# Layer 1's mixer: modulation by width quarters, part of the projections in unsplit fp32, pooling as band products

## The reference

```
mod = silu(c) @ w_ada + b_ada                    # 2048 -> 12288, one row of c
sh1, sc1, gt1, sh2, sc2, gt2 = split(mod, 6)
h = rmsnorm(x, g) * (1 + sc1) + sh1
proj = h @ w_in                                  # 2048 -> 3072
xr, gr, xp = proj[:, :1024], proj[:, 1024:2048], proj[:, 2048:]
xr = causal_dwconv(xr, w_conv, b_conv)           # 4 taps
r, i = sigmoid(xr by heads @ w_rg_a + b), sigmoid(xr by heads @ w_rg_i + b)
a = exp(8 * r * log_sigmoid(lam)); u = sqrt(1 - a*a) * i * xr
hr = scan over tokens of (a, u)
y_lru  = hr * gelu(gr)
y_pool = ((causal mean of xp over 2, 4, 8, 16 tokens) - xp) by groups @ w_pool * ls_pool
x = x + gt1 * (concat(y_lru, y_pool) @ w_out)    # 2048 -> 2048
h = rmsnorm(x, g2) * (1 + sc2) + sh2             # then the gated feed-forward, width 5632
```

## Time and profile before

| | us |
|---|---|
| median of 3 runs (2688.2 to 2691.19) | 2690.42 |
| the profiled execution's own time | 2695.73 |
| its span | 2694.0 |
| PE busy in the span | 2485.4 (92%) |
| DVE busy | 1874.6 (70%) |
| ACT busy | 1140.8 (42%) |
| POOL busy | 257.4 (10%) |
| DMA | 639.05 MB, mean 237 GB/s |

### The profile page before, as it was taken

One profiled execution on the slowest core, in us unless ns is written; L12 is line 12 of the kernel. 1 busy time (PEld: TensorE's weight loads), 2 busy tenths in 40 slices (PEclk: granted clock), 3 DMA queues, 4 the chain that ended last, 5 costly groups with the idle time before them and its releaser, 6 DMA issues.

```text
span 2694.0 us, 34697 instructions
## 1 busy us (share of the span) xinstructions
PE 2485.4 (92%) x13534; PEld 2160.7 (80%) x13534; DVE 1874.6 (70%) x1808; ACT 1140.8 (42%) x1303; POOL 257.4 (10%) x418
## 2 busy tenths in 40 slices
PE   1189788999999999999999999888999999999999
PEld 1188767888888888888999998787888888888887
DVE  5778788788888888767776445765578755555565
ACT  2053533534433443455335555433454444444443
POOL 2312611011111111100110000000001000000000
PEclk9599899999999999999999999999999999999999
DMA  9887778688888888855995555234568755555554
GB/s 333 297 303 258 257 271 311 223 308 322 308 307 307 309 307 302 286 188 172 343 324 172 163 166 157 80 116 149 197 229 306 251 189 187 190 193 193 187 181 148
DMA packets 290575, 639.05 MB, mean 237 GB/s; under 512 B 21754, under 2 KB 34556, under 8 KB 290076
## 3 DMA queue, kind: packets, MB, share of 16 engines
q1 hardware_dynamic: 236112, 440.61, 48.6%
q0 software_dynamic: 53792, 196.63, 20.0%
q10 hardware_dynamic: 556, 0.18, 0.0%
HBM read 635.28 MB, written 2.10 MB: 237 GB/s over the span
## 4 chain that ended last, share of the span: by engine, by line
PE 80%; DVE 9%; DMA 4%; ACT 2%; issue 2%; POOL 2%; DVEq 0%; POOLq 0%; ACTq 0%
PE PS L1569 79%; DMA R<-in_w_ada 4%; DVE R L964 3%; DVE WLO L944 2%; ACT WHI L516 1%; DVE R L1463 1%; POOL YF L461 1%; PE PS L1745 1%; POOL YF L460 0%; PE PS L1710 0%; POOL YF L465 0%; DVE H L989 0%; POOL R L467 0%; DVE R L1291 0%; DVE R L1032 0%
## 5 line engine op out<-in xcount | busy, mean ns | idle before, releaser
L944 DVE TENSOR_TENSOR WLO<-RAW,WHI 128x1024 fp32r<-128x1024 f32 x816 | 1004.2, 1233 | 695.3 <-ACT WHI L516 693.3
L516 ACT ACTIVATE WHI<-RAW 128x1024 fp32r<-128x1024 f32 x816 | 863.3, 1060 | 1247.8 <-PE PS L1569 1247.5
L1569 PE MATMUL PS<-WHI,H 128*128 128x512 f32 x3488 | 1088.9, 393 | 29.8 <-DVE WLO L944 19.2
L1569 PEld LDWEIGHTS PS<-WHI,H 128*128 128x128 f32 x3488 | 654.1, 189 | 172.1 <-issue 22.2
L1569 PE MATMUL PS<-WLO,H 128*128 128x512 f32 x1744 | 682.9, 392 | 0.0
L1569 PE MATMUL PS<-H,WHI 128*128 128x256 f32 x3168 | 593.7, 289 | 42.3 <-DVE WLO L944 36.4
L1569 PEld LDWEIGHTS PS<-H,WHI 128*128 128x128 f32 x3168 | 503.8, 196 | 52.9 <-DVE WLO L944 43.7
L964 DVE SCALAR_TENSOR_TENSOR R<-R,CA 128x1024 f32<-128x1024 f32 x360 | 464.9, 1291 | 46.5 <-DMA R<-in_w_ada 40.6
L1569 PE MATMUL PS<-H,WLO 128*128 128x256 f32 x1584 | 454.1, 287 | 0.0
L1569 PE MATMUL PS<-WHI,HID 128*128 128x512 f32 x1280 | 395.8, 390 | 0.0
L1569 PEld LDWEIGHTS PS<-WLO,H 128*128 128x128 f32 x1744 | 329.6, 189 | 69.7
(11 more groups left out here) (196 smaller groups left out, 1038.1 us busy)
## 6 DMA issues: line engine op xcount, KB each, us to landing
R<-in_w_ada POOLq DMA_DIRECT2D x368, 512.0 KB, 6.2
RAW<-in_w_in SPq DMA_DIRECT2D x88, 1024.0 KB, 5.5
RAW<-in_w_ffn_in SPq DMA_DIRECT2D x88, 1024.0 KB, 5.1
RAW<-in_w_ffn_gate SPq DMA_DIRECT2D x44, 1024.0 KB, 6.7
RAW<-in_w_ffn_up SPq DMA_DIRECT2D x44, 1024.0 KB, 5.3
RAW<-in_w_ffn_down SPq DMA_DIRECT2D x44, 1024.0 KB, 8.1
RAW<-in_w_ffn_out SPq DMA_DIRECT2D x44, 1024.0 KB, 5.1
RAW<-in_w_out SPq DMA_DIRECT2D x32, 1024.0 KB, 6.1
```

The costliest lines, as they stand in the source:

```text
L516: nc.scalar.activation(WHI[j][:, :, :], RAW[slot][:, 2 * half:2 * half + 2, :], ACT.Copy)\
L944: nc.vector.tensor_tensor(WLO[j][:, :, :], RAW[slot][:, 2 * half:2 * half + 2, :], WHI[j][:, :, :].bitcast(F32), ALU.subtract).then_inc(lo ...
L1569: return nc.tensor.matmul(o, a, b, start=start, stop=stop, skip_group_check=True)
```

## The change

Four things change in block 1's first half; everything from the feed-forward on keeps its work.

1. *Modulation by width quarters.* The first 64 ada loads are grouped by quarter of the width (512 columns of sh1 and the same 512 of sc1, in runs of 2 KB instead of 4 KB), into eight slots instead of four. As soon as a quarter's sum is there, that quarter of `h` is formed. The 96 loads after them go into four slots, all by POOL's queue.
2. *Half the input projection per quarter, unsplit.* For each quarter PE multiplies three units (both column groups of xr, the first of xp) directly from `RAW` in fp32; the quarters add up in the PSUM pairs A, B and C. The other 12 units are split in three as before. A native unit needs no `hi` and no `lo`; its slot is freed by PE.
3. *Output projection unsplit.* All 16 units are multiplied in fp32, from `YF`. The order of the units changes: first the rows of the pooling part. DVE and ACT split nothing there. Of 96 later ada loads DVE takes 20 beside the 24 split subs and 76 after them.
4. *Pooling as band products.* DVE builds small band matrices once; PE multiplies xp by them. POOL computes nothing any more in the mixer.

```diff
...
+NATIVE = ((0, 24), (2 * U_WOUT1, 2 * U_FFN1))
+def native_before(s):
+    return sum(max(0, min(s, last) - first) for first, last in NATIVE)
+W_OUT1 = [(0, 2), (0, 3), (1, 2), (1, 3), (2, 2), (2, 3), (0, 0), (0, 1), (1, 0), (1, 1), (2, 0), (2, 1),
+          (3, 2), (3, 3), (3, 0), (3, 1)]
+W_OUT1_PAIR = "BACB"
...
-ADA_BEFORE_W_OUT = 4
-ADA_BESIDE_W_OUT = [[] for _ in range(32)]
-ADA_SUM_IN_W_OUT = {}
...
+ADA_IN_W_IN = {s: 1 for s in (0, 1, *range(6, 24))}
+ADA_FIRST = sum(ADA_IN_W_IN.values())
+SUM_IN_W_IN = {22: 4}
+SUM_IN_W_OUT = {9: 5, 17: 6, 23: 7, 30: 8}
...
             def slot_free():
-                if c.unit.at >= 4:
-                    sp.wait_ge(lo_done, c.unit.value(-3, times=2))
+                last = 2 * (c.unit.at - 4)
+                if any(first <= last < end for first, end in NATIVE):
+                    sp.wait_ge(pe_sub, last + 2)
+                elif last >= 0:
+                    sp.wait_ge(lo_done, c.unit.value(-3, times=2) - native_before(last))
                 c.unit.at += 1
                 return (c.unit.at - 1) % 4
...
-            for col in (0, 2 * LRU):
+            sp.wait_ge(ada_op, 4)
+            for q in range(4):
+                for col in (0, COLS, 2 * LRU):
+                    load(w_in, 4 * q, col)
+            for col in (2 * LRU + COLS, LRU, LRU + COLS):
                 group(w_in, col)
-                group(w_in, col + COLS)
-            c.ada.at = SP_GROUP * KT
-            for u in range(8):
-                load(w_in, 4 * (u % 4), LRU + u // 4 * COLS)
-                for k in (2 * u, 2 * u + 1):
-                    sp.wait_ge(ada_op, c.ada.value(-3))
-                    sp.dma_start(ADA[c.ada.at % 4], ada_w[0][:, k, SP_GROUP * ADA_COLS:(SP_GROUP + 1) * ADA_COLS])\
-                        .then_inc(ada_in_sp[c.ada.at % 4], 16)
-                    c.ada.at += 1
-            for g in range(4):
-                group(w_out, g * COLS)
+            for g, q in W_OUT1:
+                load(w_out, 4 * q, g * COLS)
             ffn(w_gate, 0, w_up, 0, w_down)
...
+            def ada_quad(q):
+                for k in range(KT):
+                    slot = c.ada.at % 8
+                    if c.ada.at >= 8:
+                        pool.wait_ge(ada_op, c.ada.value(-7))
+                    pool.dma_start(ADA[slot].rearrange("p (w n) -> p w n", w=2),
+                                   ada_w[0][:, k, :].rearrange("p (w n) -> p w n", w=6)[:, 0:2, q * 512:(q + 1) * 512])\
                         .then_inc(ada_in[slot], 16)
                     c.ada.at += 1
...
-            for g in range(4):
-                ada(0, g * ADA_COLS)
+            for q in range(4):
...
-            def window(g):
-                src = R[:, 16 + 2 * g:18 + 2 * g, :]
-                cur, w = src, 2 << g
-                for level in range(g + 1):
-                    dst, s = sums[level % 2], 1 << level
-                    step(pool.tensor_copy(dst[:, :, 0:s], cur[:, :, 0:s]))
-                    step(pool.tensor_tensor(dst[:, :, s:T], cur[:, :, s:T], cur[:, :, 0:T - s], ALU.add))
-                    cur = dst
-                inv = BASE[:, INV + 16 * g:INV + 16 * g + w]
-                for a in range(2):
-                    step(pool.tensor_tensor(cur[:, a, 0:w], cur[:, a, 0:w], inv, ALU.mult))
-                step(pool.tensor_scalar(cur[:, :, w:T], cur[:, :, w:T], 1.0 / w, 1.0, ALU.mult, ALU.mult))
-                pool.tensor_tensor(src, cur, src, ALU.subtract).then_inc(pooled, 1)
-                pool.wait_ge(pooled, g + 1)
...
-            for g in range(4):
-                window(g)
-            pool.wait_ge(rg_sig, 16)
-            pool.wait_ge(conv_step, 24)
-            pool.tensor_tensor(tiles(40, 8), tiles(40, 8), tiles(24, 8), ALU.mult).then_inc(ix_done, 1)
-            c.ada.at += KT
-            for b in (7, 8, 9, 10, 11):
+            for b in (4, 5, 6, 7, 8, 9, 10, 11):
                 ada(0, b * ADA_COLS)
...
+                step(nc.vector.memset(yf[:, 0:5 * WIDE], 0.0))
+                step(nc.vector.tensor_copy(BAND[0][:, 16:16 + P], ident))
+                for g in range(4):
+                    s = 1 << g
+                    step(nc.vector.tensor_tensor(BAND[g + 1][:, 16:], BAND[g][:, 16:], BAND[g][:, 16 - s:WIDE - s], ALU.add))
+                for g in range(4):
+                    first = BASE[:, INV + 16 * g:INV + 16 * g + 16]
+                    for out_, w in ((RIGHT[g], P), (LEFT[g], 144)):
+                        step(nc.vector.scalar_tensor_tensor(out_, BAND[g + 1][:, 16:16 + w], 1.0 / (2 << g),
+                                                            BAND[0][:, 16:16 + w], ALU.mult, ALU.subtract))
+                    step(nc.vector.tensor_tensor(LEFT[g][:, 0:16], BAND[g + 1][:, 16:32], first, ALU.mult))
+                    ins = nc.vector.tensor_tensor(LEFT[g][:, 0:16], LEFT[g][:, 0:16], ident[:, 0:16], ALU.subtract)
...
+            for g in range(4):
                 for kt in range(KT):
                     ada(kt, 0, (ACC, G)[g % 2])
-                    if kt == 3:
-                        ada_end()
-            lo(2)
-            ada_end()
-            modulation(COL["g_norm_mix"], mod_at(0, 1), 4)
-            split_affine(XT)
-            win_body(0, skip=2)
+                    if g == 0 and kt == 9:
+                        dve.wait_ge(prm_t, 1)
+                        nc.vector.tensor_copy(PRM[:, :], MISC[:, 0:BLOCKS * P]).then_inc(prm_ready, 1)
+                        mean_squares(0, 4)
+                        normed()
+                    if g and kt == 2:
+                        modulation_quad(g - 1)
+                    if g and kt == 9:
+                        split_affine(g - 1)
+                    if g == 1 and kt == 12:
+                        window_bands()
+                    if g == 2 and kt == 12:
+                        dve.wait_ge(lam_done, 1)
+                        step(nc.vector.scalar_tensor_tensor(SM[:, 0:8], PRM[:, COL["lru_lambda"]:COL["lru_lambda"] + 8],
+                                                            0.0, SM[:, 8:16], ALU.min, ALU.subtract))
+                        nc.vector.tensor_scalar(SM[:, 0:8], SM[:, 0:8], 8.0, None, ALU.mult).then_inc(c8_done, 1)
+            modulation_quad(3)
+            split_affine(3)
+            c.unit.at, c.sub.at = 12, 24
+            rest = iter(ADA_REST)
+            def ada_rest():
+                n, kt = next(rest)
+                ada(kt, 0, (ACC, G)[n % 2])
+                if n > 5 and kt == 3:
+                    ada_end()
...
+            for s in range(24):
                 lo()
-                ada_beside(0, s, 16)
-                if 3 <= s < 11:
-                    convolution(s - 3)
...
-            lo(2)
+                if 2 <= s < 6:
+                    convolution(2 * (s - 2))
+                    convolution(2 * (s - 2) + 1)
+                for _ in range(ADA_IN_W_IN.get(s, 0)):
+                    ada_rest()
+            ada_end()
+            dve.wait_ge(a_done, 8)
...
+            step(nc.vector.tensor_tensor(tiles(40, 8), tiles(40, 8), tiles(24, 8), ALU.mult))
+            for _ in range(4):
+                ada_rest()
             dve.wait_ge(root_done, 1)
-            dve.wait_ge(ix_done, 1)
             step(nc.vector.tensor_tensor(tiles(40, 8), tiles(40, 8), tiles(32, 8), ALU.mult))
             for t in range(8):
                 ins = nc.vector.tensor_tensor_scan(R[:, 24 + t, :], R[:, t, :], R[:, 40 + t, :], 0.0, ALU.mult, ALU.add)
             step(ins)
             dve.wait_ge(gelu_done, 1)
+            dve.wait_ge(pooled_mm, 2)
             for q in range(2):
                 nc.vector.tensor_tensor(YF[:, 4 * q:4 * q + 4, :], R[:, 24 + 4 * q:28 + 4 * q, :],
                                         R[:, 8 + 4 * q:12 + 4 * q, :], ALU.mult).then_inc(yf_quad, 1)
...
-            split()
+            for _ in range(12):
+                ada_rest()
             dve.wait_ge(ada_bias, 6)
             diagonals(0, mod_at(0, 2))
...
-                        lo()
-                    if g and s == 1:
-                        residual("BA"[g % 2], 0, g - 1, 4 + g // 3)
-                    for n, kt in ADA_BESIDE_W_OUT[8 * g + s]:
-                        if kt < KT:
-                            ada(kt, 0, (G, ACC)[n % 2])
-                        else:
-                            ada_end()
+            def residual_of(n, last, freed):
+                dve.wait_ge(pe_sub, 2 * U_WOUT1 + last + 1)
+                pair = W_OUT1_PAIR[n]
+                gated(PAIR[pair][:, :, :], 0, n).then_inc(free[pair], 1)
+                dve.wait_ge(free[pair], freed)
+                add_gated(0, n)
+            for _ in range(12):
+                ada_rest()
+            residual_of(0, 15, 3)
+            for _ in range(8):
+                ada_rest()
+            residual_of(1, 19, 4)
+            for _ in range(8):
+                ada_rest()
+            residual_of(2, 23, 2)
+            for _, _ in ADA_REST[ADA_FIRST + 44:]:
```

(62 more changed lines are left out.)

349 lines of the change are left out of this document (183 added, 166 removed).

## The result

The changed kernel takes 2651.41 us (median of 4 runs, 2650.53 to 2656.45), the kernel before 2690.81 us on the same chip (4 runs, 2688.2 to 2694.8). The ratio is 0.9856, 95% interval 0.9839 to 0.9874: 39.4 us less, where I had forecast some 30 (2661 us). The profiled execution took 2651.49 us.

What follows compares the result with a forecast made beforehand. An opening alternating between DMA working while PE waits and PE working while DMA has slack was taken as the bound. Stage times put the first feed-forward product at 438, not 467.6: 2690.4 - 29.6 = 2661 us, range 2638 to 2688.

Steps and rivals of the forecast that it cites:

- first quarter's sum: Opening: 16 ada loads and four units, 14.7 MB; bounds 37 and 50 us, taken as 44.
- second to fourth: Three later quarters: 16 loads and three units each, 11.5 MB at 380 GB/s, 30.4 us each; last load multiplied at 136.
- last native unit of the quarters ends: Input projection, twelfth unsplit unit: 136 + 6.2 for steps + 21.4 of PE + 2.4 for the low clock = 166.
- split half and pooling products end: Input projection, 12 split units: 67.5 us, plus gate, pooling and band products, convolutions and waits; sum 96, ending at 262.
- mixer outputs on DVE: After the split units: DVE's squaring, combination, products, four ada, scan and outputs, from 258.5 to 282.
- last sum: Output projection: 72 ada multiplications paced by a four-slot ring of loads; 282 + 5.6 + 90 + 44.5 + 2 = 424.
- first feed-forward product: Boundary: sum at low clock 3.6, chain 9.3, low clock 1 more; 438 instead of 467.6, 29.6 earlier.
- The bands: Quarters, DVE: 22 small steps adding 4 to 11 us once, mostly hidden by eight slots; 1 us charged.
- rival C: Four native pieces in the quarters: PE stays at 1.2 GHz, 42.8 us each; +55, 2716 us; chance 2%.
- rival B: Quarters: ring of eight fails, loads keep 295 GB/s; 26 us lost, 2687 us; chance 13% with its shades.
- the restart: Quarters: after PE's pause of about 8 us the clock is low for some 5 us of work; 2.4 charged.
- the two kinds of interval: Output projection: 43 ada loads at 2.1 us beside streaming units, then 25 alone at 1.78 us.

Runs made afterwards that it cites:

- the sums first: The changed kernel with TensorE doing all four modulation sums of the quarters before its first product, undoing the overlap: 2703.53 us, ratio 1.0047 to the kernel before.

## Why the prediction was right

By its steps, in us from the span's start:

| step | forecast | measured |
|---|---|---|
| first quarter's sum | 44 | 39.8 |
| second to fourth | 74, 105, 136 | 75.2, 103.6, 131.3 |
| last native unit of the quarters ends | 166 | 158 |
| split half and pooling products end | 262 | 250.5 |
| mixer outputs on DVE | 282 | 266.1 |
| last sum | 424 | 412.0 |
| first feed-forward product | 438 | 424.9 |

**Right in mechanism.** The quarters run at 387 GB/s from 50 to 120 us (forecast 380) with three native units beside each 16 loads; the three later quarters take 91.6 us in all (92). They are not alike, as I had them: 35.5, 28.3 and 27.8 us. The bands hold DVE for 6.6 us in the first of the three (64.5 to 71.1), and it then finds loads waiting until 84.8. PE waits ahead of group 7's sum (9.7 us) and at the end (27.3 us) for DVE, which waits for loads. There is no wait at group 8's sum, which I had named: PE's piece from sum to sum is 32.9 us, and 16 loads at 2.03 us are 32.5. That the two are so near is chance. That PE stays at 1.2 GHz (rival C) did not come: after a pause the 64 instructions take 16.7 or 15.5 us, where they take 13.98 at full clock (the sums first). The four-slot run is rival B made real, and cost 19 us where I had priced 26 for the three later quarters; of these it lost 9.2 there, and 7.3 in the first quarter, for which I had priced nothing. With it a clear gain would have stayed.

**Off in size**, all but one to the late side, 13 us in all by the first feed-forward product:
- First quarter, -4.2. I took 44 between bounds of 37 and 50, near the 42.4 of the same loads in four slots, and gave the eight slots nothing here. With four the changed kernel's first sum comes at 47.0, with eight at 39.8. By then 14.2 MB were moved, at 356 GB/s. The three quarters behind it: -0.4.
- After the fourth quarter, -3.3. The first product starts 4.5 us behind the sum instead of 6.2: the sum itself takes 1.95 us at full clock, where the kernel before had it at the low clock in 3.57, and the steps behind it are as long as before (2.6 us). The three units take 22.3 us instead of 23.8. At full clock the 64 instructions of two units of 256 columns take 13.8 us from their start to the next, and one of 512 columns 6.9, so a unit is 6.9 us either way (I had 7.14 either way). The piece behind the fourth sum needs 15.4 for the first two, with the granted clock at 0.66 from 135 to 140 us: the restart costs 1.6, where I charged 2.4.
- Split half, -3.6 (92.4 us for 96), and the steps to the outputs, -4.4 (15.6 us for 20). Inside the first, the two convolutions per sub held DVE at 4.0 us per sub (I had 4.4), which is 1.6 us in four subs; the other 2 are not broken down. In the second, DVE starts 6.1 us ahead of PE's last product (244.4 for 250.5; I had 3.5) and needs 21.7 us where my terms make 23.6: I had priced two steps at 3.1 us that now take 2.29. In the kernel before the first of them takes 3.12 us, with POOL's sums beside it, and 2.28 when these are left out.
- Output projection, +4: 146 us from the outputs to the last sum against 142. The 72 loads average 2.03 us where my terms average 1.97; which of the two kinds of interval was short I did not separate. One term was mis-added too: fourteen units are 14.7 MB, not 14.2, which moves the sum by 1 us.
- Boundary, -1.1.

The misses before the outputs and the +4 behind them cancel in part, which is luck. So is some of the agreement in the medians: the profiled run of before lay 5 us above its median, so the forecast is 14.6 us off in the profiled spans (29.6 for 44.2) and 9.8 in the medians (29.6 for 39.4).

**What the gain is made of.** The quarters' overlap is necessary: without it the change loses (the sums first, +52 us). Of VectorE's freed time, 39 us in the output projection are worth 11 us in the new order, and the pooling is worth at most 13 us in the old one; the parts interact and do not add up to the 39.4. My sentence that DVE's 56 dropped splits gain "nothing beyond this sum" was right for the order of events and wrong as a judgement of worth: with the time of 32 splits put back the ring slows. Whether split products with their ACT part would cost more than 11 us stays open; that was not tried.

The rule that I had weighed (the Trainium skill, "DMA: Bandwidth & Descriptors", Queues, rings and completion order) is that each engine takes turns between the queues by whole packets. The trace fits it while both queues are full: from 24 to 34 us the eight-slot kernel moves 687 packets of one and 685 of the other. What did not hold is what I made of it. I had expected equal shares of the bytes, all 6.3 MB of the other queue within the first 16 loads, and a first sum at 47. In the profile's count a packet of the ada queue carries 3.6 KB (2.50 MB in 687) even with runs of 2 KB, one of the units 2.0 KB, and by 40 us the other queue had moved 4.86 MB. With four slots the turns are uneven, 547 to 963 packets: I take it that the ada queue then runs empty at times, which no view shows directly.

## What to carry to other kernels

If a profile shows a stage in which loads run and TensorE waits, followed by one where TensorE runs and loads have slack, put one beside the other before making either cheaper: here that decided 52 us, and in the output projection the dearer products of TensorE cost nothing. Then ask what ends the stage (here the last load, shown by halving the products for no change) and move its loads to where the rate is low: twelve loads moved in a table gave 18 us, more than the pooling's 13 at most. Count the slots of a ring against its round trip, but expect from more slots only what lies between the present rate and the one at a DMA share of 1 (here 364 and 395 GB/s, 10 us). And take the price of an instruction from rows at one clock: the same 32 products take 15.4 or 13.8 us here for the clock alone.

## What the runs showed of the hardware

- Loads of 0.5 MB from one queue, beside units of 1 MB from another: four in flight 335 GB/s, eight 387 (50 to 120 us). In the output projection 364 and 395. A load's median time from issue to landing went from 5.8 to 11.8 us and from 6.4 to 13.5: it doubled for rates that rose by 16 and 8%.
- Halving a load's bytes at four in flight took its landing from 6.4 to 4.0 us, so by a straight line through the two, an estimate, 1.6 of the 6.4 us do not go with the bytes (6.4 less twice the 2.4 saved). The 72 loads then averaged 1.82 us instead of 2.03.
- An fp32 product at full clock took 0.43 us with 256 moving columns (13.81 us for 32, the sums first) and 0.86 us with 512 (6.87 for 8): per column the two forms cost the same, and the units of the output projection run at 6.9 us each as well. The 15.5 to 16.7 us that the same 32 take in the changed kernel hold a piece at the low clock: the granted clock is 0.50 from 40 to 50 us, 0.82 from 50 to 60 and 1.00 from 60 to 70, where TensorE had paused for 4.9 us and begun again at 48.1.
- Two queues that are both full took turns by packets of unequal size: 687 packets with 2.50 MB against 685 with 1.37 MB in 10 us.
